# SBUF tensors on multiples of 64 bytes, the last head's chunks in another order, and feed's splits and sums moved, in a hybrid transformer layer

## The reference

```python
# x: (1, 2048, 1024) float32, one layer
h = rms_norm(x, attn_norm_g)
qd, kd, vd, qr, fr, ir, gr = split(h @ w_in)            # seven parts of 512 columns
od = diff_attention(norm(qd) * 64**-0.5, norm(kd), vd, lam)   # 4 heads: softmax map 1 - lam * softmax map 2, block-causal
od = rms_norm(od, subln_g) * (1 - lam_init)             # per head and row
orr = hgrn2_chunked(silu(qr), 1 - sigmoid(fr), ir, log_sigmoid(fr))  # 4 heads of 128, gated recurrence
orr = rms_norm(orr, hgrn_norm_g) * silu(gr)
x = x + concat(od, orr) @ w_out
h = rms_norm(x, ffn_norm_g)
x = x + (silu(h @ w_gate) * (h @ w_up)) @ w_down        # d_ff = 2816
```

## Time and profile before

| | us |
|---|---|
| median of 3 runs | 2775.96 (2774.65 to 2776.91) |
| profiled execution | 2776.23 |
| its span, first to last instruction | 2774.5 |
| mean TensorE clock granted | 0.982 |

### The profile page before, as it was taken

How to read it: one execution, slowest core, us unless ns; L and a number is a source line. 1 busy time by engine, 2 the same in 40 slices (tenths; PEclk the granted TensorE clock), 3 DMA queues, 4 the chain that set the end, 5 groups by cost and what they waited for, 6 DMA issues and landing times. The chain is left out here.

```text
span 2774.5 us, 34306 instructions
## 1 busy us (share of the span) xinstructions
PE 2634.8 (95%) x13288; PEld 2214.1 (80%) x13288; DVE 1557.5 (56%) x1906; ACT 1131.1 (41%) x1922; POOL 896.2 (32%) x607
## 2 busy tenths in 40 slices
PE   7999999999999999986998999998999997999999
PEld 6888888887888888875776888886888885888887
DVE  5434344333676767656677565657666664356653
ACT  4434344332567666674444222224222222332231
POOL 5001100002424242303556454555454451135400
PEclk9999999999999999997998999999999998999999
DMA  4755555384343433315675334345333333777763
GB/s 154 257 181 198 172 192 198 121 282 130 100 112 102 112 101 84 92 35 197 227 254 187 98 101 111 99 114 178 110 103 104 95 102 119 260 274 266 250 208 127
DMA packets 343874, 430.48 MB, mean 155 GB/s; under 512 B 19232, under 2 KB 212768, under 8 KB 341024
## 3 DMA queue, kind: packets, MB, share of 16 engines
q1 hardware_dynamic: 343712, 428.29, 49.2%
HBM read 301.87 MB, written 129.50 MB: 155 GB/s over the span
## 5 line engine op out<-in xcount | busy, mean ns | idle before, releaser
L522 DVE TENSOR_TENSOR proj_w_lo<-proj_w_raw,proj_w_hi 128x2048 fp32r<-128x2048 f32 x56 | 129.8, 2318 | 233.6 <-ACT proj_w_hi L422 233.6
L2142 PE MATMUL down_prod<-down_w_hi,down_f_hi 128*128 128x512 f32 x616 | 241.2, 391 | 19.8 <-DVE down_f_lo L2078 18.9
L669 PE MATMUL proj_prod<-proj_w_hi,proj_h_lo 128*128 128x512 f32 x640 | 251.5, 393 | 0.0
L2143 PE MATMUL down_prod<-down_w_lo,down_f_hi 128*128 128x512 f32 x616 | 240.3, 390 | 0.0
L2144 PE MATMUL down_prod<-down_w_hi,down_f_lo 128*128 128x512 f32 x616 | 240.1, 390 | 0.0
L1621 ACT ACTIVATE feed_a_hi<-lend_shared 128x1024 fp32r<-128x1024 f32 (+1 forms) x78 | 94.1, 1207 | 325.7 <-PE feed_v_bank L1869 162.5
L1015 ACT ACTIVATE att_expo<-att_ring,att_neg_max 128x1024 f32<-128x1024 f32 (+4 forms) x192 | 164.8, 862 | 92.7 <-DVE att_neg_max L1126 74.0
L2048 ACT ACTIVATE down_f_hi<-down_f_raw 128x768 fp32r<-128x768 f32 x112 | 83.0, 786 | 281.8 <-PE down_prod L2144 279.0
L1621 ACT ACTIVATE feed_a_hi<-feed_full 128x1024 fp32r<-128x1024 f32 (+1 forms) x78 | 94.0, 1205 | 236.8 <-PE feed_y_bank L1869 155.2
L1867 PE MATMUL feed_y_bank<-feed_b_hi,feed_a_hi 128*128 128x512 f32 x416 | 165.7, 398 | 17.8 <-DVE feed_results L1748 17.8
L1867 PE MATMUL feed_x_bank<-feed_b_hi,feed_a_hi 128*128 128x512 f32 x416 | 163.2, 392 | 12.7 <-DVE lend_lent L1717 12.7
(11 more groups left out here) (254 smaller groups left out, 6860.4 us busy)
## 6 DMA issues: line engine op xcount, KB each, us to landing
proj_w_raw<-in_w_in_dram SPq DMA_DIRECT2D x56, 1024.0 KB, 6.5
lend_shared<-in_w_gate_dram SPq DMA_DIRECT2D x88, 256.0 KB, 4.1
feed_full<-in_w_up_dram SPq DMA_DIRECT2D x88, 256.0 KB, 4.1
ff<-feed_results SPq DMA_DIRECT2D x88, 256.0 KB, 2.6
down_w_raw<-in_w_down_dram SPq DMA_DIRECT2D x22, 1024.0 KB, 7.9
down_f_raw<-ff SPq DMA_DIRECT2D x56, 384.0 KB, 3.3
down_f_raw<-ff SPq DMA_DIRECT2D x56, 320.0 KB, 3.6
ff<-feed_ff_sum SPq DMA_DIRECT2D x66, 256.0 KB, 3.2
```

Of the source, the lines that this page charges most:

```text
L522: nc.vector.tensor_tensor(w_lo[n % 2][:], w_raw[n % 2][:], w_hi[n % 2][:].bitcast(F32), ALU.subtract).then_inc(w_lo_made, 1)
L669: last = pe.matmul(prod[t][:], lo[:, s, tile], wh[:, k, :], start=False, stop=stop)
L2142: pe.matmul(dst, hi[:, s, :], wh[:, s, :], start=opens and s == 0, stop=False, skip_group_check=True)
L2143: pe.matmul(dst, hi[:, s, :], wl[:, s, :], start=False, stop=False, skip_group_check=True)
```

## The change

Three groups of edits.

1. `Alloc.sb` puts a filler of 32 bytes behind every tensor that takes an odd number of 32-byte lines, so that all tensors start on multiples of 64 (all of `project`, `mix_tokens`, `feed`, `down`).
2. In `mix_tokens` the first eight fills of a head alternate between the fill bank and the ring's last bank, with the ring at three banks for a head's first four steps. Of the last head, chunks 0 and 4 are normalised by ACT in step 63 and turned and taken at step 64; the other six (5, 6, 7, 1, 2, 3) are scaled by DVE (`normalise_late`) and taken at step 65. The roots of rows 0 to 11 are taken in step 63, those of rows 12 to 15 at step 65. POOL waits for group 0's quadrants and sums them at the end of the stage; SP loads these after chunk 0.
3. In `feed` two b's (not three) are split ahead of a set; in a set's first group the others are split at pos 0 (two), 1, 2 and 3 and the next group's a at pos 4, and POOL's sums there wait until all seven are split. At pos 0 `root`s stand ahead of `high(g, 2)` on ACT, and `use(g - 1, TILE12)` ahead of `low(g, 2)` on DVE in all groups. In group 8 slabs are turned after pos 3 and 4. SP's `store_quads` and `store_t` go to pos 5 and 6.

```diff
     def sb(self, name, shape, dt=F32):
-        return self.ctx.enter_context(self.nc.sbuf_tensor(f"{self.prefix}_{name}", shape, dt))
+        tensor = self.ctx.enter_context(self.nc.sbuf_tensor(f"{self.prefix}_{name}", shape, dt))
+        size = math.prod(shape[1:]) * (1 if dt == mybir.dt.uint8 else 4)
+        if -(-size // 32) % 2:
+            self.ctx.enter_context(self.nc.sbuf_tensor(f"{self.prefix}_{name}_fill", [P, 8], F32))
+        return tensor
...
+def sum_quadrants(nc, pool, f, made, done):
+    nc.gpsimd.tensor_tensor(f[:, AT_S1], f[:, AT_A21], f[:, AT_A22], ALU.add).then_inc(made, 1)
...
 def mix_tokens
+    SPARE = RING - 1
+    SPARE_FILLS = 2 * GROUP
...
     for s in range(TOTAL):
+        banks = SPARE if s % STEPS < GROUP else RING
+        if s % STEPS == GROUP:
+            at = SPARE - 1
         for m in range(2):
             runs[s, m], key, left = [], 0, (s % STEPS + 1) * P
             while left:
-                n = min(RING - at, RUN_BANKS, -(-left // 512))
+                at %= banks
+                n = min(banks - at, RUN_BANKS, -(-left // 512))
...
+    LAST_CHUNKS = (0, *range(TURNS, CHUNKS), *range(1, TURNS))
+    LATE_CHUNKS = LAST_CHUNKS[2:]
+    LAST_TAKEN = {TOTAL: LAST_CHUNKS[:2], TOTAL + 1: LATE_CHUNKS}
+    LAST_ROOTS = TOTAL - 1
+    EARLY_ROWS = STEPS - GROUP
...
+            pool.wait_ge(first_full_in, 64)
+            sum_quadrants(nc, pool, first_full, first_summed, 0)
...
+                if s == LAST_ROOTS:
+                    take_roots(HEADS - 1, EARLY_ROWS)
...
                 if s == TOTAL + 1:
-                    normalise(HEADS - 1, 0)
+                    take_row_roots(HEADS - 1, EARLY_ROWS, STEPS)
...
+                if s == LAST_ROOTS:
+                    invert_roots(HEADS - 1, EARLY_ROWS)
+                if s == TOTAL:
+                    for c in LATE_CHUNKS[:-1]:
+                        normalise_late(c)
+                if s == TOTAL + 1:
+                    invert_last_roots()
+                    normalise_late(LATE_CHUNKS[-1])
...
+                    if (s, m, n) == first_spare[s // STEPS]:
+                        pe.wait_ge(fill_read, filled(s // STEPS, SPARE_FILLS - 1))
...
             def fill(h, n):
                 kind, side, at = FILLS[n]
-                if filled(h, n) > 1:
-                    pe.wait_ge(fill_read, filled(h, n) - 1)
+                out = bank_of(n)
+                if n == 1:
+                    if h:
+                        pe.wait_ge(exp_made, spare_free[h])
+                elif filled(h, n) > 2:
+                    pe.wait_ge(fill_read, filled(h, n) - (2 if 0 < n < SPARE_FILLS else 1))
...
 def feed
-        EARLY = 3
+        EARLY = 2
+        LATE = {0: (2, 3), 1: (4,), 2: (5,), 3: (6,)}
...
 gpsimd
-            sums(0)
             for g in range(GROUPS):
+                if opens_set(g):
+                    pool.wait_ge(b_lo_made, OPERANDS * (set_of(g) + 1))
                 if g + 1 < GROUPS:
                     sums(g + 1)
...
 scalar
                     if pos == 0:
-                        high(g, 2)
-                        if is_up(g):
-                            sigmoid(g - 1, TILE12)
                         if p is not None:
                             root(p, 1, TILE22)
                             root(p, 0, TILE12)
-                    if opens_set(g) and pos + EARLY < OPERANDS:
-                        high_b(set_of(g), pos + EARLY)
+                        if not opens_set(g):
+                            high(g, 2)
+                        if is_up(g):
+                            sigmoid(g - 1, TILE12)
...
+                    if opens_set(g):
+                        for i in LATE.get(pos, ()):
+                            high_b(set_of(g), i)
+                        if pos == 0:
+                            high(g, 2)
-                    if pos == 2 and g + 1 < GROUPS:
+                    if pos == (4 if opens_set(g) else 2) and g + 1 < GROUPS:
                         high(g + 1, 0)
...
 vector
                     if pos == 0:
                         if g:
                             make_c12(g - 1)
-                        if p is not None:
-                            use(p, TILE12)
-                        low(g, 2)
-                        if g and p is None:
                             use(g - 1, TILE12)
-                    if opens_set(g) and pos + EARLY < OPERANDS:
-                        low_b(set_of(g), pos + EARLY)
+                        if not opens_set(g):
+                            low(g, 2)
                     if pos == 1 and p is not None:
                         scale(p, 1)
                         scale(p, 0)
                     if pos == 2:
                         make_u2(g)
-                        if g + 1 < GROUPS:
-                            low(g + 1, 0)
+                    if opens_set(g):
+                        for i in LATE.get(pos, ()):
+                            low_b(set_of(g), i)
+                        if pos == 0:
+                            low(g, 2)
                     if pos == 4:
                         make_v2(g)
                         make_c21(g)
-                        if g + 1 < GROUPS:
-                            low(g + 1, 1)
+                    if pos == (4 if opens_set(g) else 2) and g + 1 < GROUPS:
+                        low(g + 1, 0)
+                    if pos == 4 and g + 1 < GROUPS:
+                        low(g + 1, 1)
```

More of the change, by code:

```diff
@@ L12 @@
+import math
 from contextlib import ExitStack
@@ L740, in mix_tokens @@
         last_in.update({x: n for x in mine})
+    spare_free = [max([0] + [RUN_AT[s, m, r] + 1 for (s, m, r) in RUN_AT if s < h * STEPS
+                             and runs[s, m][r][0] <= SPARE < runs[s, m][r][0] + -(-runs[s, m][r][2] // 512)])
+                  for h in range(HEADS)]
+    first_spare = {h: min((s, m, r) for (s, m, r) in RUN_AT if s >= h * STEPS
+                          and runs[s, m][r][0] + -(-runs[s, m][r][2] // 512) > SPARE) for h in range(HEADS)}
     MAX_RUNS = max(len(rs) for rs in runs.values())
@@ L814, in mix_tokens @@
         fill_bank = r.bank("fill")
+        fill_banks = [fill_bank[:], ring[:, SPARE * 512:(SPARE + 1) * 512]]
         small_in = early.small_in
@@ L859, in filled, with bank_of @@
             return h * len(FILLS) + n + 1
+        def bank_of(n):
+            return fill_banks[n % 2 if n < SPARE_FILLS else 0]
         def fill_at(*key):
@@ L1172, in invert_roots, with invert_last_roots, normalise_late @@
                 dve.wait_ge(o_rms_made, h + 1)
-                nc.vector.reciprocal(o_rrms[:], o_rms[:]).then_inc(o_rrms_made, 1)
+                nc.vector.reciprocal(o_rrms[:, 0:rows], o_rms[:, 0:rows]).then_inc(o_rrms_made, 1)
+            def invert_last_roots():
+                dve.wait_ge(o_rms_made, HEADS + 1)
+                nc.vector.reciprocal(o_rrms[:, EARLY_ROWS:], o_rms[:, EARLY_ROWS:]).then_inc(o_rrms_made, 1)
+            def normalise_late(c):
+                h = HEADS - 1
+                if c < TURNS:
+                    dve.wait_ge(o_rrms_made, HEADS + (c == TURNS - 1))
+                    dve.wait_ge(o_squared, h * STEPS + (c + 1) * GROUP)
+                    for t in range(c * GROUP, (c + 1) * GROUP):
+                        nc.vector.tensor_scalar(o_all[h % 2][:, t, :], o_all[h % 2][:, t, :], o_rrms[:, t:t + 1], None,
+                                                ALU.mult).then_inc(late_scaled, 1)
+                else:
+                    dve.wait_ge(r_rrms_made, HEADS)
+                    dve.wait_ge(r_gated, HEADS)
+                    head = c - TURNS
+                    for t in range(CH):
+                        part = ro[:, t, head * C:(head + 1) * C]
+                        at = t * HEADS + head
+                        nc.vector.tensor_scalar(part, part, ro_rrms[:, at:at + 1], None, ALU.mult).then_inc(late_scaled, 1)
             nc.vector.memset(state[:], 0.0)
@@ L1271, in fill @@
                         tok = slice(c * C, (c + 1) * C)
-                        last = pe.matmul(fill_bank[:, tok], rk[:, head, tok], rq[:, head, tok], start=True, stop=True)
+                        last = pe.matmul(out[:, tok], rk[:, head, tok], rq[:, head, tok], start=True, stop=True)
                 elif kind == "level":
@@ L1870, in _ @@
                     last.then_inc(prod_done, 1)
-                    if p is not None and pos in (2, 3):
-                        turn_slab(p, 2 * (pos - 2))
-                        turn_slab(p, 2 * (pos - 2) + 1)
+                    if p is not None and pos + 1 in turned_after(g):
+                        s = 2 * turned_after(g).index(pos + 1)
+                        turn_slab(p, s)
+                        turn_slab(p, s + 1)
 def down(nc, ff, w_down, x_mid, y, stored):
```

93 lines of the change are left out of this document (50 added, 43 removed).

## The result

The changed kernel takes 2783.79 us (median of 9 runs, 2779.47 to 2784.95) against 2775.96: 1.0022 times as long, 95% interval 1.0011 to 1.0032. It is slower, where 15 us less were forecast, and the time lies above the range. The profiled execution has a span of 2782.1, 7.6 more than before.

The account below looks back on a forecast made before the run. PE, busy 95% of the span, was taken to bound the kernel, through its waits and slow matmuls. -13.3 - 6.6 - 4.1 - 4.0 + 12.5 + 0 + 2 - 1.5 = -15.0 gave 2761 us, range 2742 to 2778.

Parts of the forecast that it names:

- Part 1: All tensors on multiples of 64 bytes: matmuls with mixed operands get faster, 7.6 us in project, 5.7 in feed; -13.3.
- Rival (a): Address doesn't matter; something else of `lent`, such as its place in memory, slows its matmuls: 2774 us; chance 18%.
- Part 2: Mixing, fills in two banks: PE's waits at fills go, less costs at step 4 and in run order; -6.6.
- The other order of runs: Mixing, steps 8 to 11 of each head: runs change places, net +0.3 a head, put at +1.
- Part 3: Last head of mixing: chunks and roots moved earlier, feed starts at 1254.2 against 1258.28; -4.1.
- part 4: Feed's opening: first matmul earlier, waits for u2 and a new one for c22; -4.0.
- Part 5: Feed's groups 1 to 7: roots ahead of high(g, 2) delay the turn, +2.5 for each of groups 2 to 6; +12.5.
- +2 for the clock: Feed: cold clock after the 4 us stalls, +2.
- Rival (c): Stalls of about 4 us in each of groups 2 to 8 let the clock fall: 2783 us; chance 10%.
- Rival (b): Part 5 costs nothing, as x lands earlier or scalings no longer meet GpSimd's sums: 2747 us; chance 22%.
- Groups 7 and 8: Feed: group 7's wait for c22 goes, group 8's wait before the turn becomes other waits; together 0.
- part 6: Feed's groups 29 and 30: a wait for c22 goes, the 8.8 becomes 4 for u2 and 4 for c22; -1.5.

Follow-up runs that it names:

- e10: Kernel before with 224-byte gaps in project and feed, making `lent_h` (`lent` as PE reads it) congruent to the other operands modulo 256: 2763.53 us, ratio 0.9944.
- e5: e1 with 448-byte gaps in project and feed, making `lent` as PE reads it congruent to the other operands modulo 512: 2753.38 us, ratio 0.9914.
- e11: e1 with the ring started at bank 0 instead of 2 in step 4 of each head: 2759.45 us, ratio 0.9932.
- e7: Changed kernel, roots still ahead of high(g, 2), with SP storing x ahead of loading the next a at pos 0: 2764.07 us, ratio 0.9951.
- e1: Changed kernel with high(g, 2) put back ahead of the two roots on ACT at pos 0: 2761.35 us, ratio 0.9941.
- e4: Kernel before with only the two roots put ahead of high(g, 2) on ACT at pos 0: 2796.48 us, run once.
- e3: Changed kernel with all tensors on multiples of 128 bytes instead of 64: 2781.18 us, ratio 1.0015.
- e9: e5 with group 8's old opening put back and x stored ahead of the loads of a, as in e7: 2744.30 us, ratio 0.9878.
- e6: e1 with 192-byte gaps, `lent` as PE reads it congruent to the rest modulo 256 but 256 apart modulo 512: 2757.8 us, one run.

## Why the prediction was wrong

**Part 1 (-13.3, measured -3.4)** is the first step that failed. The observation was right, mixed operands cost, and so was the size: e10 gives 7.9 in project and 0.11 a group, against 7.6 and 0.11. What failed is "the change puts everything on 64" as if that made the operands lie alike. The blocks and operands of the earlier trace rows showed only pairs 32 apart and pairs alike; that 64 is enough was assumed. The addresses that follow from the sizes have lent_h 64 off the others modulo 128 after the change, and that was not asked. Rival (a), `lent`'s own place, fell with e5. The rule weighed there ("TensorE: Matmul & The Clock Gate", section "Step-by-step: what each phase is for", of the Trainium skill: two independent read ports, weight loads take nothing from the running matmul) would have made all these kernels alike. They aren't, by 13.5 us in e10, so the measurement decides against reading it as "addresses don't matter"; what happens at the ports no run shows.

**Part 2 (-6.6, measured -3.4).** The waits at fills went, and the first eight steps of the heads gained 6.0 of the 7.6 forecast for them: PE waits in their stead, among others, for DVE at the turns in step 3 of each head (0.7) and in step 1 of head 0 (1.3). The other order of runs was put at +1 and cost 3.1 (0.8 a head, e11): one run per step was counted, whereas four runs and a turn wait differently. That the clock fell in other heads took 0.6 off.

**Part 3 (-4.1, measured -4.8)** and **part 4 (-4.0, measured -4.0)** held as sums; no run takes either apart, and of their terms these can be read. ACT's taking of chunks waits for the stores (4.01), and feed opens as worked out, first matmul 5.3 us after the first load (5.3 forecast), a wait for u2 of 4.6 (4.1) and the new one for c22 of 2.4 (3.2). ACT, SP and PE, end of mixing and group 0:

```profile
1239.57 0.69 ACT L1083 ACTIVATE att_stage<-att_turned,early_rg_col 128x512 f32<-128x512 f32 x1 [4.01 <-DMA mix<-att_stage]
1246.63 0.32 SPq L160 DMA_DIRECT2D feed_b_lo<-out_operands  x1
1251.97 0.76 PE L1961 MATMUL feed_x_bank<-feed_b_hi,feed_a_hi 128*128 128x512 f32 x1 [9.62 <-DVE lend_lent L1811]
1266.79 0.77 PE L1961 MATMUL feed_y_bank<-feed_b_hi,feed_a_hi 128*128 128x512 f32 x1 [4.64 <-DVE feed_results L1842]
1280.32 0.47 PE L1961 MATMUL feed_v_bank<-feed_b_hi,feed_a_hi 128*128 128x512 f32 x1 [2.38 <-DVE feed_results L1860]
```

**Part 5 (+12.5, and +2 for the clock; measured +20.4 in groups 2 to 6).** The sign was right, and DVE's wait of 2.93 for high and, in group 4, PE's of 3.9 at the turn stand there as forecast. Counting intervals of PE's matmuls beyond 227 ns, the stalls of the five groups grew from 6.4 to 19.8 us: +13.4, near 12.5, but as 7, 1.5, 4, 1.6, 6 and not as 4 each. That the sum is near is luck: the prediction named the store and load of x behind low(g, 2) and then took x to be no later than before, which left out the loop through SP that makes x late in every other group (e7). The term that was mis-sized is the clock: matmuls slower than at full clock cost 7.9 us there instead of 0.9, 2.3 to 2.9 after each of the three long stalls. With group 8 (6.8 instead of 3.4), and less the one fall of group 7 before (1.7), which is gone, the clock took 8.7 us more than before, where 2 were put down. Rival (c) named this and gave nearly the measured time, 2783, but with falls in all of groups 2 to 8; groups 3, 5 and 7 had none and group 8 had one already before, and the rest of the distance to the forecast is parts 1 and 2. That the number agrees is luck. Rival (b), that the order costs nothing, fell with e1 and e4.

**Groups 7 and 8 (0, measured +4.4), part 6 (-1.5, measured -1.5).** The length of the stalls in group 8 was near (11.4 before, 12.3 after), and again the clock wasn't: one long stall became three. Part 6 held as a sum.

The sum of the differences to the forecast: 9.9 (part 1) + 3.2 + 0.9 (stalls) + 5.0 (clock) + 4.4 (group 8) less 0.8 = 22.6, which is 7.6 + 15.0. The range left no room for it because it left rival (c) out, whose own time of 2783 lies above it, and because a small part 1 and the falls of the clock were taken as cases apart, while both came in part.

## What to carry to other kernels

When tensors are aligned to speed up matmuls, work out the addresses of the two operands of each pair and make them congruent, here modulo 256 bytes; a gap of 224 bytes in each of two stages did what rounding every tensor to 64 did not. Before an instruction is put ahead of another on an engine whose result a DMA's issue waits for, follow the loop through that DMA to the next use of its buffer: here 2.5 us in a loop with no slack came back as 5 to 8 in every other round, and moving one store ahead of the loads gave the loop its slack. And price an idle stretch of PE with the clock that follows it: in group 8 three stalls of the same sum cost 3.9 us more of PE's busy time than two that lay together.

## What the runs showed of the hardware

- In feed's steady groups a 128x512 matmul starts 226 to 227 ns after the one before it when all of PE's operands are congruent modulo 256 bytes (e5), and up to 236 when `lent` is 64 off the rest (the changed kernel), 235 at 32 off (before), 234 at 128 off (e3); the pattern repeats every few matmuls, and at 64 off it lasts for nine matmuls into operands that agree.
- After PE had idled 3.94 us the granted clock fell from 1.0 to 0.5 of full speed, the level of 1.2 GHz: the eight transposes at 1369.05 took 1.97 us, those at 1343.93, after 1.33 us of idling, 1.09. Idle times of 1.8 to 2.3 us were followed by a fall in some places (1.8 ahead of `v_bank` in group 7 of e9) and not in others (2.3 at the turn of group 7 of e10). At the turns of groups 2 to 6 1.61 was followed by one in e6, and 1.65 and 1.83 in e1 were not: the length of an idle stretch alone did not tell.
